# Later steps in the up and down stages of a two-layer trunk: SP's writes, GELU, splits, folds and flips one to three chunks on

## The reference

```
D_MODEL = 2048; SEQ = 256; D_FF = 5632
def conv_ffn(h, w_up, conv_w, conv_b, w_down):
    u = causal_dwconv(h @ w_up, conv_w, conv_b)      # width 3, over tokens
    gate, val = jnp.split(u, 2, axis=-1)
    return (jax.nn.gelu(gate) * val) @ w_down
for l in range(2):
    ...
    x = x + conv_ffn(rmsnorm(x, norm_ffn[l]), ffn_w_up[l], ffn_conv_w[l], ffn_conv_b[l], ffn_w_down[l])
```

## Time and profile before

| | us |
|---|---|
| median of 3 runs | 2174.16 |
| lowest, highest | 2173.91, 2175.26 |
| the profiled execution | 2174.17 |
| its span | 2172.4 |
| TensorE matmul busy | 2163.4 |
| VectorE, ScalarE busy | 1701.7, 1362.7 |

### The profile page before, as it was taken

One profiled execution on the slowest core, in us unless ns is written; L12 is line 12 of the kernel. 1 busy time (PEld: TensorE's weight loads), 2 busy tenths in 40 slices (PEclk: granted clock), 3 DMA queues, 4 the chain that ended last, 5 costly groups with the idle time before them and its releaser, 6 DMA issues.

```text
span 2172.4 us, 28550 instructions
## 1 busy us (share of the span) xinstructions
PE 2163.4 (100%) x9780; PEld 1797.1 (83%) x9780; DVE 1701.7 (78%) x1968; ACT 1362.7 (63%) x1950; POOL 16.5 (1%) x48
## 2 busy tenths in 40 slices
PE   9999999999999999999999999999999999999999
PEld 8888888888888888888888888888888888887887
DVE  7877866788888886887776676577888888868875
ACT  6554445678787777645555555556777777766553
POOL 2000000000000000000000000000000000000000
PEclk9999999999999999999999999999999999999999
DMA  7666667777777777666676687576777777776774
GB/s 277 215 211 212 197 199 235 217 237 244 250 248 239 244 257 238 209 218 216 228 244 202 232 263 242 186 221 217 256 234 258 234 247 235 258 250 201 236 252 149
DMA packets 269357, 500.15 MB, mean 230 GB/s; under 512 B 18928, under 2 KB 56832, under 8 KB 269136
## 3 DMA queue, kind: packets, MB, share of 16 engines
q1 hardware_dynamic: 267408, 492.78, 70.5%
q0 software_dynamic: 1424, 5.60, 0.7%
q10 hardware_dynamic: 432, 0.56, 0.1%
HBM read 457.15 MB, written 41.71 MB: 230 GB/s over the span
## 4 chain that ended last, share of the span: by engine, by line
PE 81%; DVE 7%; DMA 5%; issue 4%; ACT 3%; SPq 0%; DVEq 0%; ACTq 0%
PE ps L1192 16%; PE ps L1193 16%; PE ps L1194 16%; PE ps L1087 6%; PE ps L1089 6%; PE ps L1088 6%; PE ps L1064 4%; DVE w_lo L1425 2%; PE ps L1098 2%; PE ps L1100 2%; PE ps L1099 2%; DMA raw<-w_up 2%; PE ps L1068 2%; DMA raw<-w_down 2%; ACT w_hi L621 1%
## 5 line engine op out<-in xcount | busy, mean ns | idle before, releaser
L1425 DVE TENSOR_TENSOR w_lo<-raw,w_hi 128x1024 fp32r<-128x1024 f32 x744 | 898.3, 1221 | 360.7 <-ACT w_hi L621 349.4
L621 ACT ACTIVATE w_hi<-raw 128x1024 fp32r<-128x1024 f32 x744 | 777.4, 1054 | 497.1 <-PE ps L1194 215.6
L1192 PE MATMUL ps<-w_hi,xs 128*128 128x512 f32 x1904 | 743.0, 390 | 0.4 <-DVE w_lo L1425 0.3
L1193 PE MATMUL ps<-w_lo,xs 128*128 128x512 f32 x1904 | 740.8, 389 | 0.0
L1194 PE MATMUL ps<-w_hi,xs 128*128 128x512 f32 x1904 | 740.8, 389 | 0.0
L1192 PEld LDWEIGHTS ps<-w_hi,xs 128*128 128x128 f32 x1904 | 357.4, 188 | 75.8 <-DVE w_lo L1425 1.7
L1194 PEld LDWEIGHTS ps<-w_hi,xs 128*128 128x128 f32 x1904 | 357.5, 188 | 74.3
L1193 PEld LDWEIGHTS ps<-w_lo,xs 128*128 128x128 f32 x1904 | 357.5, 188 | 73.4
L1087 PE MATMUL ps<-w_hi,act 128*128 128x512 f32 x736 | 287.0, 390 | 0.7 <-DVE w_lo L1425 0.6
L1089 PE MATMUL ps<-w_hi,act 128*128 128x512 f32 x736 | 286.4, 389 | 0.0
L1088 PE MATMUL ps<-w_lo,act 128*128 128x512 f32 x736 | 286.4, 389 | 0.0
(11 more groups left out here) (312 smaller groups left out, 1974.3 us busy)
## 6 DMA issues: line engine op xcount, KB each, us to landing
raw<-w_up SPq DMA_DIRECT2D x352, 512.0 KB, 4.5
raw<-w_in SPq DMA_DIRECT2D x191, 512.0 KB, 4.4
raw<-w_down SPq DMA_DIRECT2D x176, 512.0 KB, 4.7
turn_line<-cross SPq DMA_DIRECT2D x284, 128.0 KB, 2.4
h<-turn_line SPq DMA_DIRECT2D x71, 512.0 KB, 4.7
raw<-w_out SPq DMA_DIRECT2D x64, 512.0 KB, 4.9
prob_line<-probs_t SPq DMA_DIRECT2D x12, 192.0 KB, 3.7
probs<-prob_line SPq DMA_DIRECT2D x3, 768.0 KB, 6.4
```

What stands on the lines that cost most here:

```text
L621: act_f(w_hi[:, s, :, :], raw[:, s, :, :], ACT.Copy).then_inc(hi_ready, 1)
L1192: mm(out, x_hi, w_hi[:, s, u, :], start=first and u == 0 and not (begun and t == 0), stop=False)
L1193: mm(out, x_hi, w_lo[:, s, u, :], start=False, stop=False)
L1425: tt(w_lo[:, s, :, :], raw[:, s, :, :], w_hi[:, s, :, :].bitcast(F32), ALU.subtract).then_inc(lo_ready, 1)
```

## The change

Only the places of steps in the written orders change; what is computed stays. In both layers: SP's four writes of each half of up go behind load 2 or 10 instead of 1 or 9 (the fetches stay behind 3 and 11; the same holds for the last pair's writes at the start of down). GELU goes from stage 17 to 18 (chunk 10 instead of 9 in the pair, behind the copy L746, which stands at chunk 10), the split of the product from stages 16 and 17 to 17 and 18. The folds' rounding goes from chunks 11 and 15 to 12 and 17, their split from 13 and 17 to 14 and 18. In layer 1's down: the second and fourth flips go from 25 and 60 to 28 and 61; SP's write of a flipped block stands 5 chunks behind its flip instead of 4, the fetch 7 instead of 6, ScalarE's copy 8 instead of 5.

```
-FLIPS = (17, 25, 52, 60)
+FLIPS = (17, 28, 52, 61)
+PUT_X, FETCH_X, COPY_X = 5, 7, 8
-FOLD_FULL, FOLD_SUMS, FOLD_HI, FOLD_LO = (8, 12), (10, 14), (11, 15), (13, 17)
+FOLD_FULL, FOLD_SUMS, FOLD_HI, FOLD_LO = (8, 12), (10, 14), (12, 17), (14, 18)
-ADDS_AT, GELU_AT, PROD_AT, SPLIT_AT = ((13, 15), (13, 14)), 17, 14, (16, 17)
+ADDS_AT, GELU_AT, PROD_AT, SPLIT_AT = ((13, 15), (13, 14)), 18, 14, (17, 18)
...
             for i, (half, p) in enumerate(UP_CHUNKS[fast]):
                 load(w_up[ph.layer], ph.q_up + 4 * j, i, bass.ds(j * NB + half * D_FF, NB), p)
-                if i % KC == 1:
+                if i % KC == 2:
                     put(ph.n_up + 2 * (j - 1) + i // KC)
...
-                if i < 2 * KC and i % KC == 1:
+                if i < 2 * KC and i % KC == 2:
                     put(ph.n_down - 2 + i // KC)
...
-                if l and i - 4 in FLIPS:
-                    put_x(FLIPS.index(i - 4))
-                if l and i - 6 in FLIPS:
-                    fetch(ph.m_down + FLIPS.index(i - 6))
+                if l and i - PUT_X in FLIPS:
+                    put_x(FLIPS.index(i - PUT_X))
+                if l and i - FETCH_X in FLIPS:
+                    fetch(ph.m_down + FLIPS.index(i - FETCH_X))
...
-                if l and i - 5 in FLIPS:
-                    x_copy(FLIPS.index(i - 5))
+                if l and i - COPY_X in FLIPS:
+                    x_copy(FLIPS.index(i - COPY_X))
```

## The result

| | us |
|---|---|
| before, median of 5 runs beside it | 2175.26 (2173.91 to 2176.17) |
| after, median of 5 runs | 2251.91 (2248.11 to 2259.27) |
| ratio | 1.0365, 95% interval 1.0352 to 1.0379 |
| profiled execution of after, its span | 2259.27, 2257.5 |

The change costs 76.7 us. The forecast was 24 (2198), and its range ended at 2218: right in direction, wrong in size.

What follows compares the result with a forecast made beforehand. TensorE was taken as full, with a second chain of equal length beside it. 2174.2 + 28.0 for late writes in up - 3.5 won = 2198.7, taken as 2198 us; own range 2182 to 2215, wider range 2171 to 2218.

Steps and rivals of the forecast that it cites:

- The loop beside TensorE: Up: a chain of waits through VectorE, loads, fetch and ScalarE takes 42.68 us a pair against TensorE's 42.83, 0.15 to spare.
- the writes behind a load: Up: SP's writes, 0.65 us behind a load, land in 3.6 us (2.5 to 4.7) instead of 2.1 to 2.5.
- Rival (a): Writes land 2.5 us after the last, as fast as now; up costs nothing, down is won: 2171 us, chance 0.15.
- Part of that comes back: Up, half 0: fetch issued 1.3 us later but travels faster, data 0.3 us later; round grows 0.6 us (0.1 to 2.0).
- half 1: Up: fetch goes 1.6 us later, load 12 1.1 later plus 0.2 travel; round grows 1.4 us (0.2 to 2.4).
- Rival (c): Up: the writes take 4.7 us, as behind two loads; round grows 4.4 us, 2237 us in all, chance 0.07.
- Pair 10 ... I cost it at nothing: Last pair of up: no shared chunk, and splits run far ahead of TensorE, so no cost.
- chunk 15 ... just enough: Layer 1's down: chunk 15 gets 0.3 us less spare, taken as just enough, so nothing is lost.
- down of layer 1: Chunks 17 to 34: moved folds and flips win back all 3.0 us lost, leaving 43.5 us.
- the wait near 1777: One up pair where TensorE loses 0.5 us, counted in the 3.5 us the change can win.
- All at nothing: Up, both layers: moved GELU, ScalarE's split of the product and VectorE's L1864 cost no time.
- if the fetch were on time: Up: then GELU alone would push chunk 12 by 0.5 us, covered by TensorE's spare.

Runs made afterwards that it cites:

- rest_only: The changed kernel with SP's writes of up and early down back behind loads 1 and 9: 2176.00 us, ratio 1.0003.
- down_only: The kernel before with all the change's lines for down except the writes (folds, flips, places of write, fetch and copy): 2172.58 us, ratio 0.9991.
- put_first: The kernel before with SP's four writes after the wait for the slot of load 2 (10) but ahead of that load: 2229.12 us, ratio 1.0260.
- half0_only: The kernel before with only half 0's writes late, behind load 2, in up and down: 2208.47 us, ratio 1.0154.
- fetch_alone: The changed kernel, but SP waits for each fetch of up to land before it loads on: 2293.84 us, ratio 1.0547.
- half1_only: The kernel before with only half 1's writes late, behind load 10, in up and down: 2207.67 us, ratio 1.0150.
- down_start: The kernel before with the change's lines for down, including late writes in its first 16 chunks; up's writes as before: 2173.75 us, ratio 0.9992.
- puts_only: The kernel before with only SP's writes moved one chunk later, in up and the first 16 chunks of down: 2257.12 us, ratio 1.038.
- fold0_back: The changed kernel with the first fold's rounding and split back at 11 and 13 in both layers: 2251.73 us, ratio 1.0365.
- gelu_only: The kernel before with only GELU at stage 18 and the product's splits at 17 and 18, both layers: 2176.12 us, ratio 1.0008.

## Why the prediction was wrong

**Right: what bounds the kernel.** The loop beside TensorE has no spare, and what is added to it comes out in TensorE's pair: 47.40 us in both. No writes late, no loss (rest_only, down_only).

**Right: the writes behind a load.** Forecast 3.6 us to landing, measured 3.6 to 3.9; put_first, without the load, 2.7. Rival (a) falls by that. The figure of about 2 us that the prediction set beside (a) from the Trainium skill (DMA: Bandwidth & Descriptors, Anatomy of one DMA) is given there for DMAs issued from GpSimd, and these writes are SP's. The fetches are issued 1.63 us later in both halves, where 1.3 and 1.6 were forecast.

**Failed: "Part of that comes back".** For half 0 the step said that a fetch with load 3 farther ahead would travel about 1 us less, so that "the data comes 0.3 us later", and took 0.6 us for the half. Alone it grows the round by 2.1 us (half0_only). The step looked at what is ahead of the fetch and took what is behind it as before. While SP waits, the slots of loads 4 and 5 come free, and with load 6 they leave as a block behind the fetch. It travels 0.9 us more instead of 1.0 less. fetch_alone, which holds these loads back, gives 1.0 us of it back.

**Mis-sized: half 1.** 1.4 us forecast, 1.9 by half1_only: its fetch travels 0.9 us more there, and I had 0.2 for a transfer. Together: 2.0 us a round forecast, 4.34 measured. The table's growth is against a mean of 43.00 us, in which TensorE itself holds some rounds back. Against TensorE's own 42.83 the round is 4.51 us too long: 16 x 4.51 = 72.2 us. Over the stretch of the sum, from the shared step of pair 1 to that of pair 9, the trace has 69.8 us, and the forecast had 28.0. The 2.4 us between are 0.8 that the kernel before loses there itself and 0.8 a layer for the first round, which the sum took off rightly. Rival (c), 2237 us, had the growth of 4.4 right, for another reason: the writes don't take 4.7 us.

**Put at nothing: what follows the last shared step.** The other 3.5 us of the 73.4 come between the shared step of pair 9 and pair 10, 1.75 a layer. No wait of TensorE lies there. Behind the wait ahead of that step its matmuls start 0.43 us apart for a while, and the loop is over, so nothing hides it (after, layer 1):

```profile
1944.46 0.50 PE L1099 MATMUL ps<-w_hi,xs 128*128 128x512 f32 x1 [2.29 <-DVE w_lo L1426]
...
1946.76 0.63 PE L1101 MATMUL ps<-w_hi,up_x_lo 128*128 128x512 f32 x1
1947.19 0.63 PE L1099 MATMUL ps<-up_hi,up_x_hi 128*128 128x512 f32 x1
```

**Failed: "Pair 10 ... I cost it at nothing", "chunk 15 ... just enough".** Both were read with the loop on time, and with the loop on time both hold (down_start). In the trace of after VectorE enters down with 2.0 us in hand at chunk 0 of layer 1 instead of 5.0 (from the end of that chunk's split to TensorE's start of it), and chunk 14 has 0.65 us instead of 2.80. In the profiled execution 14.5 us are lost there over both layers, of which 3.6 lie ahead of chunk 14 in layer 0. A late loop alone doesn't do it: in puts_only and fold0_back, with loops as late, layer 0 enters with 2.0 and 1.8 us and loses 4.1 up to chunk 17, but layer 1 enters with 4.6 and 4.5 and loses nothing. What sets the time in hand there, and how this loss is spread over the runs of after, whose median lies 7.4 below the profiled one, stays open.

**Right in place and size, but not in cause: down of layer 1.** Chunks 17 to 34 take 2111.36 - 2067.84 = 43.52 us in after (43.53 forecast). The second fold wins 2.9 of the 3.0 us with no flip moved; the flips alone weren't tried. The sum took off 3.5 us, 0.5 more, for the wait near 1777. No step of it says why that should be won, and no run shows it: up of layer 1 is 0.2 us longer in down_only and 2.7 in rest_only.

**Not settled: "All at nothing" for GELU and the splits.** With late writes, as in the change, nothing speaks against it: after isn't slower than puts_only (2251.91 and 2257.12 us), and both have rounds of 47.1 to 47.4 us. With the writes on time, rest_only stands at 2176.00 and down_only at 2172.58, each beside its runs of before (1.0003 and 0.9991). By the medians GELU and the splits take back what down wins, but the two intervals overlap, and gelu_only's takes in no change. The forecast named 0.5 us "if the fetch were on time" and gave it to TensorE's spare; that spare is neither shown nor refuted.

## What to carry to other kernels

When a step on a queue that feeds the whole kernel waits longer, look at what becomes ready behind it meanwhile: it leaves as a block, and the transfer that everybody waits for shares the engines with it. Price a moved DMA by the transfers close ahead of it and close behind it (here up to some 2 us), not by its own old duration. Where a loop has as little spare beside a full engine as the 0.15 us here, a step moved into idle time isn't free until it is timed: down_only and down_start, which leave GELU and the splits alone, are the only kernels here whose median is 2 us below the one before. And a place read as "just enough" in the old profile should be read again with the lateness that the forecast itself adds.

## What the runs showed of the hardware

Means over 16 rounds each: a 512 KB fetch on this queue travels 3.25 us with the nearest load 3.3 us ahead and 1.2 behind, 4.57 with loads 0.64 ahead and 0.64 behind, 5.47 with one 2.3 us ahead and three within 1.9 behind, 6.13 with two ahead at 0.65 and 2.4 and one behind at 0.7. A load issued 0.6 us behind a fetch takes 6.2 us, and 3.4 with the fetch landed. That transfers slow those issued before them (5.47 against 4.50) was what I hadn't counted on. How much isn't set by the block behind alone: with the same three loads within 1.9 us behind but the load ahead at 2.95 us, the fetch of half 1 takes 3.91, against 3.67 with nothing behind. The Trainium skill's page DMA: Bandwidth & Descriptors (Issuing engines are not separate DMA queues) says that all DMAs run on the same 16 engines and interleave there; the trace agrees, for a single queue as well.

After some waits, of 2.6 and 3.5 us among them, TensorE's granted clock fell for a while: 0.67 over 2060.6 to 2064.8, with matmuls 0.43 us apart, that is 1.2 GHz instead of 2.4. The matmuls just behind the wait still run at the full pace (2060.96 to 2061.89, 0.23 apart), and the fall comes a microsecond or more later. Behind the wait of 2.89 us at 1613.24 it didn't come: the granted clock is 1.00 over 1614 to 1620. Inside the loop I read the slow stretches as hidden, since the loop sets the pace; behind the last shared step of each layer and in down they cost 1.7 to 1.8 us each.
